# Finer modulation units in the opening, and two modulation sums moved from ahead of the attention to behind it

## The reference, cut to what matters

```python
ml = (silu(c) @ mod_w[i] + mod_b[i])            # 6 * 1024 columns a layer
sh1, sc1, g1, sh2, sc2, g2 = split(ml, 6)
hl = xl * (1 + sc1) + sh1                       # latent tokens; hc likewise with c_ctx
q, k, v = split(h @ wqkv, 3)                    # rotary turn of q and k (latent)
y = diff_attention(q, k, v) @ wo                # 8 heads, two softmaxes a head
x = layer_norm(ALPHA * x + (1 + g1) * y)
x = layer_norm(ALPHA * x + (1 + g2) * moe(x * (1 + sc2) + sh2))
```

## Time and profile before

| | |
|---|---|
| median of 3 runs | 1204.79 us (1202.83 to 1206.70) |
| the profiled execution | 1203.59 us |
| its span | 1201.6 us, 12396 instructions, granted PE clock 0.985 |
| PE busy | 1134.2 us (94%) |
| DVE busy | 362.4 us (30%) |
| ACT busy | 166.6 us (14%) |
| read from memory | 476.18 MB, 397 GB/s over the span |

### The profile page before, as it was taken

How to read it: one execution, slowest core, us unless ns; L and a number is a source line. 1 busy time by engine, 2 the same in 40 slices (tenths; PEclk the granted TensorE clock), 3 DMA queues, 4 the chain that set the end, 5 groups by cost and what they waited for, 6 DMA issues and landing times.

```text
span 1201.6 us, 12396 instructions
## 1 busy us (share of the span) xinstructions
PE 1134.2 (94%) x5288; PEld 494.0 (41%) x5288; DVE 362.4 (30%) x732; ACT 166.6 (14%) x397; POOL 8.0 (1%) x10
## 2 busy tenths in 40 slices
PE   8997998898999999999999889999999999988986
PEld 3553554545444333343333227543333433333322
DVE  1559999673111121111111115212111111111113
ACT  1101233614100000001000005200000100000000
POOL 0000000000000000000000010000000000000000
PEclk9998999899999999999999999999999999999998
DMA  9999896983999999999999999999999999999994
GB/s 397 403 361 368 301 361 261 402 323 155 431 430 430 431 429 429 432 430 431 431 430 430 430 427 427 424 431 430 431 430 430 431 430 431 431 428 432 430 429 181
DMA packets 40441, 480.17 MB, mean 400 GB/s; under 512 B 5056, under 2 KB 6336, under 8 KB 8384
## 3 DMA queue, kind: packets, MB, share of 16 engines
q1 hardware_dynamic: 39328, 476.91, 94.6%
q10 hardware_dynamic: 1056, 2.43, 0.7%
HBM read 476.18 MB, written 1.05 MB: 397 GB/s over the span
## 4 chain that ended last, share of the span: by engine, by line
PE 69%; DMA 23%; DVE 6%; ACT 1%; issue 1%; another core or an unknown queue 0%; DVEq 0%; SPq 0%; ACTq 0%
PE ps L913 41%; DMA ring<-in_moe_wu 12%; DMA ring<-in_moe_wg 8%; PE ps L905 4%; PE ps L921 4%; DMA ring<-in_mod_w 3%; PE ps L662 3%; PE ps L762 2%; PE ps L665 2%; DVE ring L1350 1%; PE ps L725 1%; PE ps L668 1%; PE ps L743 1%; DVE modp L1350 1%; PE ps L578 1%; PE ps L931 1%
## 5 line engine op out<-in xcount | busy, mean ns | idle before, releaser
L913 PE MATMUL ps<-ring,tra 128*64 128x512 f32 x2048 | 454.1, 597 | 24.2 <-DMA ring<-in_moe_wu 19.2
L913 PEld LDWEIGHTS ps<-ring,tra 128*64 128x64 f32 x2048 | 147.5, 138 | 322.6 <-issue 280.8
L913 PE MATMUL ps<-ring,work 128*64 128x512 f32 x1024 | 226.8, 595 | 1.9 <-DVE work L1701 1.9
L913 PEld LDWEIGHTS ps<-ring,work 128*64 128x64 f32 x1024 | 71.6, 137 | 135.6 <-issue 133.3
L1240 ACT ACTIVATE work<-ps 128x512 f32<-128x512 f32 x32 | 19.1, 598 | 506.7 <-PE ps L913 506.7
L1699 DVE TENSOR_TENSOR work<-work,ps 128x512 f32<-128x512 f32 x32 | 22.0, 688 | 206.0 <-PE ps L913 206.0
L1233 ACT ACTIVATE tra<-ps,cols 128x128 f32<-128x128 f32 x128 | 48.2, 457 | 255.1 <-PE ps L905 255.1
L1696 DVE TENSOR_TENSOR work<-ps,work 128x512 f32<-128x512 f32 x32 | 22.1, 692 | 202.3 <-ACT work L1240 202.3
L905 PEld LDWEIGHTS ps<-extra,xn 128*128 128x128 f32 x512 | 61.0, 195 | 24.3 <-issue 22.7
L905 PE MATMUL ps<-extra,xn 128*128 128x128 f32 x512 | 66.9, 285 | 1.4 <-DVE extra L1609 1.4
L921 PE MATMUL ps<-work,extra 64*128 64x512 f32 x256 | 63.6, 615 | 1.6 <-DVE work L1705 1.6
(11 more groups left out here) (191 smaller groups left out, 730.2 us busy)
## 6 DMA issues: line engine op xcount, KB each, us to landing
ring<-in_moe_wg SPq DMA_DIRECT2D x64, 2048.0 KB, 29.8
ring<-in_moe_wu SPq DMA_DIRECT2D x63, 2048.0 KB, 29.8
ring<-in_moe_wd SPq DMA_DIRECT2D x63, 2048.0 KB, 30.0
ring<-in_mod_w SPq DMA_DIRECT2D x40, 1024.0 KB, 9.6
ring<-in_mod_w SPq DMA_DIRECT2D x4, 2048.0 KB, 18.2
ring<-in_attn_wqkv SPq DMA_DIRECT2D x4, 2048.0 KB, 11.3
ring<-in_attn_wo SPq DMA_DIRECT2D x2, 2048.0 KB, 10.9
ring<-in_tokens SPq DMA_DIRECT2D x2, 1024.0 KB, 16.1
```

The source lines that it names most:

```text
L913: last = mm(ps[SLOTS * h:SLOTS * h + SLOTS, b, :], lhs(k0 + k), w[:, k, h * NB:(h + 1) * NB], start=(k0 + k == 0), stop=(k0 + k == KT - 1) ...
```

## The change

- The first four modulation units no longer hold shift or scale of half of the features but both of a quarter (`shift_and_scale`). Tokens and first key unit are loaded in quarters, each behind its modulation unit. PE runs `quarter_group(g, part)` for the key groups 0 to 3, with the next unit's `mod_parts` and `mod_columns` between them; the query groups 4 and 5 follow whole.
- `EARLY_SUMS` is 6 instead of 8, the ten step sums are now 6 to 15, and four (16 to 19) stand behind the attention: 16 ahead of `job_out(3)`, 17 and 18 ahead of `job_out(4)`, 19 in `attention_norm`, where `rows_sum(1)` was; that one moves into `route`. Both first rotations stand ahead of sum 5.
- `row_batch` 1, 2 and 3 go behind the groups 13 and 17 and into step 11, `row_batch(4)` behind `project(1, 1)`.
- `LOADS` is reordered from ("wo", 0) on; five units of the first expert and one of the second are issued from it, between the loads of the last sums. Slots 1 and 3 change places in `FREE`.

```diff
-FREE = (10, 4, 8, 5, 9, 6, 7, 2, 3, 1, 0)
+FREE = (10, 4, 8, 5, 9, 6, 7, 2, 1, 3, 0)
-BATCH_AT = {6: 0, 10: 1, 15: 2, 19: 3}
-EARLY_SUMS = 8
+BATCH_AT = {6: 0, 13: 1, 17: 2, 21: 3}
+EARLY_SUMS = 6
 STEP_SUMS = 10
+ROPES_AT = 5
 LOADS = [("q", 0), 0, 1, ("v", 0), 2, "rows", 3, 4, ("k", 1), 5, 6, 7, 8, ("q", 1), 9, "ahead", 10, 11, 12, ("v", 1), 13, 14,
-         ("wo", 0), 15, 16, 17, ("wo", 1), "x", 18, 19]
-AHEAD = 1
+         ("wo", 0), 15, ("wo", 1), "x", 16, 17, ("e", 1), ("e", 2), ("e", 3), ("e", 4), ("e", 5), 18, ("e", 6), 19]
+AHEAD, ISSUED = 1, 7
+def shift_and_scale(w):
+    import numpy as np
+    quarters = w[:, 0:2 * D].reshape(D, 2, 4, D // 4).transpose(0, 2, 1, 3).reshape(D, 2 * D)
+    return np.concatenate([quarters, w[:, 2 * D:]], 1)
...
-            for unit in (("mod", 0), ("mod", 2), ("k", 0), ("mod", 1), ("mod", 3)):
-                load_early(unit)
+            for i in range(4):
+                load_early(("mod", i))
+                c0, c1 = i * UNIT // 4, (i + 1) * UNIT // 4
+                load(slot(4)[:, c0:c1], tokens[:, c0:c1], sem(f"tokens_loaded_{i}"))
+                load(slot(0)[:, c0:c1], attn_wqkv[2][:, c0:c1], sem(f"first_loaded_{i}" if i < 3 else "early_loaded_0"))
...
-                elif v in (7, 8):
-                    sp.wait_ge(sem("half_summed"), 2 * (NSUM - 8 + v))
-                elif v < RING:
-                    sp.wait_ge(sem("unit_used"), NA - RING + v + 1)
+                elif v in (7, 9):
+                    sp.wait_ge(sem("half_summed"), 2 * (NSUM - 1 if v == 7 else NSUM))
+                elif v in (8, 10):
+                    early_used(sp, ("wo", (v - 8) // 2))
...
             mod_parts(0)
             keep_clock(7, 1)
             mod_columns(0)
-            keep_clock(7, 3)
-            mod_parts(1)
-            keep_clock(7, 1)
-            mod_columns(1)
-            keep_clock(4, 2)
+            keep_clock(5, 3)
...
+            for part in range(4):
+                quarter_group(0, part)
+                quarter_group(1, part)
+                if part < 3:
+                    mod_parts(part + 1)
+                quarter_group(2, part)
+                if part < 3:
+                    mod_columns(part + 1)
+                quarter_group(3, part)
+            for g in range(4, 10):
+                group(g)
...
-            row_batch(4)
-            NT_BANK = (4, 6, 5, 7)
+            NT_BANK = ((4, 6, 5, 0), (4, 6, 5, 7))
             project(1, 0)
             turn_normed(0, 0)
             project(1, 1)
-            pe.wait_ge(sem("rows_ready"), 2)
+            row_batch(4)
...
             for n in range(EARLY_SUMS):
-                if n == 6:
-                    rope_batch(0)
+                if n == ROPES_AT:
+                    for batch in range(2):
+                        rope_batch(batch)
                 unit_sum(n)
-            rope_batch(1)
...
+            unit_sum(NSUM - 4)
             job_out(3)
             heads_variance(1)
             norm_heads(1)
-            for n in range(EARLY_SUMS + STEP_SUMS, NSUM):
-                unit_sum(n)
+            unit_sum(NSUM - 3)
+            unit_sum(NSUM - 2)
             job_out(4)
...
                     if t == 0:
-                        rows_sum(1)
+                        unit_sum(NSUM - 1)
```

More of the change, by code:

```diff
@@ L52 @@
 BAND = P + 8
-PHASE_A = ([("mod", m) for m in (0, 2, 1, 3)]
+PHASE_A = ([("mod", i) for i in range(4)]
            + [(k, j) for j in range(2) for k in ("k", "q", "v")] + [("wo", 0), ("wo", 1)])
@@ L150, in laid_out @@
     given["router_w"] = router.reshape(P, KT * 32)
-    given["mod_w"] = np.stack([in_units(w) for w in given["mod_w"]])
+    given["mod_w"] = np.stack([in_units(shift_and_scale(given["mod_w"][0])), in_units(given["mod_w"][1])])
     w = given["attn_wqkv"][0]
@@ L437, in load_early @@
                 s, _ = EARLY[unit]
[L438 to L444, removed]
-            for unit in (("mod", 0), ("mod", 2), ("k", 0), ("mod", 1), ("mod", 3)):
-                load_early(unit)
+                load(slot(s), src, sem(f"early_loaded_{s}"))
+            for i in range(4):
[3 more added lines that the diff above has]
+                load(slot(0)[:, c0:c1], attn_wqkv[2][:, c0:c1], sem(f"first_loaded_{i}" if i < 3 else "early_loaded_0"))
             load(small9[:, 0:512], rope, sem("attn_small_loaded"))
@@ L505, in load_expert @@
             def load_expert(layer, e):
-                for n in range(AHEAD if layer == e == 0 else 0, EU):
-                    load_unit(layer, e, n)
+                for n in range(EU):
+                    if first_unit(layer, e) + n >= ISSUED:
+                        load_unit(layer, e, n)
             for what in LOADS:
@@ L516, in _ @@
                     load(xn[:, :].rearrange("p (t n) -> p t n", t=TT), x[0].rearrange("(t p) n -> p t n", p=P), sem("x_loaded"))
+                elif isinstance(what, tuple) and what[0] == "e":
+                    load_unit(0, what[1] // EU, what[1] % EU)
                 elif isinstance(what, tuple):
@@ L610, in mod_parts @@
                         k = 4 * r + g
-                        last = mm(bank((0, 1, 4, 5)[i], 32 * g, 32 * g + 32), cs[:, 32 * k:32 * k + 32], w[:, k, :],
+                        last = mm(bank(4 + i % 2, 32 * g, 32 * g + 32), cs[:, 32 * k:32 * k + 32], w[:, k, :],
                                   start=(r == 0), stop=(r == 1), skip_group_check=True)
@@ L615, in mod_columns @@
             def mod_columns(i):
-                bk = (2, 3, 6, 7)[i]
+                bk = 6 + i % 2
                 pe.wait_ge(sem("modp_copied"), i + 1)
+                if i >= 2:
+                    pe.wait_ge(sem("hcol_ready"), i - 1)
                 for q in range(4):
@@ L670, in multiply, with quarter_group @@
                 return last
[L672 to L676, removed]
-                else:
[L678 to L682, removed]
+            def quarter_group(g, part):
+                if part < 3:
+                    pe.wait_ge(sem(f"first_loaded_{part}"), 16)
+                else:
+                    early(("k", 0))
+                pe.wait_ge(sem("lat_ready"), 2 * part + 2)
+                pe.wait_ge(sem("ctx_ready"), 2 * part + 2)
+                for k in range(2 * part, 2 * part + 2):
                     last = multiply(g, k)
-                if part == 1:
+                if part == 3:
                     finish(g, last)
@@ L1089, in _ @@
                 turn_weights().then_inc(sem("sw_turned"), 1)
+                if layer == 0:
+                    pe.wait_ge(sem("rows_ready"), 2)
                 gather(7, 1).then_inc(sem("gather_done"), 1)
@@ L1312, in _ @@
             dve.wait_ge(sem("hbias_loaded"), 16)
[L1314 to L1319, removed]
+            v_.tensor_scalar(hb[:, 1], hb[:, 1], 1.0, None, ALU.add).then_inc(sem("hbias_ready"), 1)
+            dve.wait_ge(sem("hbias_ready"), 1)
             for i in range(4):
-                m = PHASE_A[i][1]
+                h, q = i // 2, 2 * (i % 2)
                 early_used(dve, PHASE_A[i])
@@ L1325, in _ @@
                     dve.wait_ge(sem("hcols_done"), i - 1)
-                v_.tensor_copy(sums[i % 2], bank((0, 1, 4, 5)[i])).then_inc(sem("modp_copied"), 1)
+                v_.tensor_copy(sums[i % 2], bank(4 + i % 2)).then_inc(sem("modp_copied"), 1)
                 dve.wait_ge(sem("hcols_done"), i + 1)
[L1328 to L1335, removed]
+                v_.tensor_tensor(hcol[:, :, h, q:q + 2, :], bank(6 + i % 2, 0, 8).rearrange("p (w q c) -> p w q c", w=2, q=2),
+                                 hb[:, :, h, q:q + 2].unsqueeze(3).to_broadcast([P, 2, 2, 2]), ALU.add).then_inc(sem("hcol_ready"), 1)
+                dve.wait_ge(sem("hcol_ready"), i + 1)
+                dve.wait_ge(sem(f"tokens_loaded_{i}"), 16)
+                for k in range(2 * i, 2 * i + 2):
+                    h_ = hT[:, k, 0:TOK]
+                    v_.tensor_scalar(h_, h_, hcol[:, 1, h, k % 4, 0:1], hcol[:, 0, h, k % 4, 0:1], ALU.mult, ALU.add)\
+                        .then_inc(sem("lat_ready"), 1)
             def half_sum(i):
@@ L1623, in route @@
                     normed_out(layer, t)
+                if layer == 0:
+                    rows_sum(1)
                 dve.wait_ge(sem("logits_done"), layer + 1)
```

23 lines of the change are left out of this document (12 added, 11 removed).

## The result

The changed kernel takes 1210.84 us in the median of 5 runs (1206.45 to 1212.06), against 1204.79 before: ratio 1.0051, 95% interval [1.0039, 1.0064]. It is slower by 0.5%. Its profiled execution has a span of 1209.7 us, 8.1 longer than before. Taken once more beside other kernels it gave 1210.26 us, ratio 1.0053 [1.0036, 1.0070].

What follows compares the result with a forecast made beforehand. The prediction took the end to hang on when the first expert starts, with transfers saturated from 300 us on. Terms of 0.7 and 1.4 us made 2.1 us later, 1206.9 us in the median; range 1200 to 1212.

Steps and rivals of the forecast that it cites:

- The likeliest case: Whole kernel: 2.1 us later than before, 1206.9 us in the median, given 44%.
- The wait named as the one that decides: PE waits 11.3 us ahead of group 16 for the load of ("v", 1).
- signs of being right: First scores near 102.6 us, ("v", 1) issued near 147.5, maximum of step 9 near 200, DVE waiting for mod_w near 246.
- Opening: From the kernel's start to the value groups: they start at 65.6 us, 3.4 earlier.
- Ahead of the attention: From value groups to first scores: scores at 102.6 instead of 113.04 us, 12 us won with the slow clock gone.
- The unit ("v", 1): Attention up to step 9: load issued at 147.5, landed at 160.7 us; all that was won is gone, and 0.7 us more.
- no wait at all: Rival ahead of group 16: the unit's issue is not bound by sum 10; 1194.2 us, chance 13%.
- The disputed landing: Load of ("v", 1) ahead of group 16: taken to land 13.2 us after issue, against 9.2 by the Trainium skill's rule.
- Steps 9 to 15: Late attention, with row_batch(3) waiting for sum 15 in step 11: taken as 0, bounds -1.5 and +1.9 us.
- Behind the attention: Last sums and projection: sum 18's load stands behind ("e", 5), so project(1, 0) starts 1.4 us later, bounds 0 and 3.5.
- Slower: the clock falls in the new gaps: Rival: PE's clock drops in both new gaps, up to 1.9 us each; 5.9 us later, 1210.7 us, chance 25%.
- the two gaps named: PE's new waits at row_batch(3) and at project(1, 0), about 2 us each.

Runs made afterwards that it cites:

- e9_copies_later: The changed kernel with the four ACT copies for the first keys held back until those for the first queries: 1203.32 us, ratio 0.9992 to the kernel before.
- e2_batch_later: The changed kernel with row_batch(0) behind group 7 instead of group 6: 1203.73 us, ratio 0.9997 to the kernel before.
- e1_v1_early: The changed kernel with the load of ("v", 1) moved in LOADS from behind sum 12 to behind sum 10: 1197.38 us, ratio 0.9955 to the kernel before.
- e11_copies_behind: The changed kernel with the four ACT copies of the second queries issued behind group 16 instead of group 15: 1207.01 us, ratio 1.0017 to the kernel before.
- the moved sums alone: The kernel before with the change's sums, rotations, collecting and load order, but its old opening by halves: 1207.45 us, ratio 1.0032 to the kernel before.
- e10_four: The changed kernel with ("v", 1) loaded earlier, row_batch(0) a group later, sums 18 and 19 loaded ahead of ("e", 5) and ("e", 6), row_batch(3) a step later: 1191.27 us.
- the study's fastest kernel: The changed kernel with ("v", 1) loaded earlier, row_batch(0) a group later, sums 18 and 19 loaded ahead of ("e", 5) and ("e", 6): 1189.21 us, ratio 0.988.

## Why the prediction was right and wrong

The likeliest case said 2.1 us later, less than the 0.3% that could be told from no change; it is 6 us later, inside the range of 1200 to 1212 and clearly slower. The wait named as the one that decides is there and is the largest; the step that failed is the one ahead of it, and that the range held is in part luck. By the prediction's own sign of being wrong, a first expert that starts more than 4 us from its old place, it was wrong: the expert starts 8.2 us later in the first profile and 5.7 in the second. Of the signs of being right the wait of some 11 us and DVE's wait for mod_w came as told, the latter 10 us later; the first scores, the issue of the unit and the maximum of step 9 are 4 to 7 us late. Up to that maximum, in the first profile, 5.8 us of the 7.4 above the forecast come from the first scores and 1.5 from the landing.

*Opening.* Forecast 65.6 us for the value groups, measured 65.66 (65.5 to 66.6 in the other traces with this opening). Right, including that the small pieces cost nothing on PE.

*Ahead of the attention: the step that failed.* "`row_batch(0)` needs sum 3, done at 70.68 + 3.11 = 73.8 us: 1.2 us of new wait", and from it first scores at 102.6 us. I had carried sum 3's end over from the kernel before as if its transfers could not be later. But the new opening finishes the key groups before it begins the query groups, where before the change the first halves of all six ran ahead of the second halves. So it moves ACT's four copies of the first keys forward by 10 us, in front of the transfers of sum 2. ACT's queue before and after the change:

```profile
62.95 2.54 ACTq L1104 DMA_DIRECT2D ring<-ring  x4
```
```profile
52.73 2.58 ACTq L1106 DMA_DIRECT2D ring<-ring  x4
```

`e9_copies_later` shows that they are the cause. Sum 3 ended at 76.6, the wait was 4.0 us (3.1 in the second profile), and PE's clock fell behind it in both: eight matmul instructions took 5.90 and 5.29 us instead of 3.60. Of the clock I had counted nothing. First scores at 108.4 and 106.3 us; without that wait 101.2 to 102.2, which is near the place forecast. In time it is worth 6.5 to 7 us (`e2_batch_later`, `e9_copies_later`): without this wait the kernel is level with the one before, at ratios 0.9997 and 0.9992.

*The unit ("v", 1).* Right in mechanism: the load goes out behind sum 10, and PE waits ahead of group 16. From the first scores to this issue I had 147.5 - 102.6 = 44.9 us; measured 45.2. The landing, taken as 13.2, was 14.7 and 13.7. The wait, forecast as 11.3, was 12.75 and 11.74. The slow clock cost 1.7 and 1.9 (forecast 1.9). `e1_v1_early` shows that this wait alone costs 12 to 13 us of time; the case "no wait at all" was false of the change, but is what the edit of one entry makes of it.

*The disputed landing.* With copies beside it 12.4 to 14.7 us in all ten traces in which the unit is issued behind sum 12, without 9.5 (`e11_copies_behind`), as the rows 12.5, 14.0 and 9.4 of the earlier trace rows had it. The rule of the Trainium skill ("DMA: Bandwidth & Descriptors", "Anatomy of one DMA"), an estimate of 9.2 us for the two transfers, agrees with the 9.5 and not with the others. The page gives it for transfers that GpSimd issues; these loads are issued by SP. The same page of the Trainium skill, under "Issuing engines are not separate DMA queues", says that transfers issued by different engines interleave on the same DMA engines, and these traces agree: with ACT's copies beside it SP's load took at least 12.4 us, without them 9.5.

*Steps 9 to 15.* Taken as 0. `row_batch(3)` waited 2.1 us; behind the wait its eight instructions took 1.89 us in the first profile (granted clock 0.53), and the full-speed 1.07 in two others, the moved sums alone and `e11_copies_behind`. The projection starts 8.7 us late where the maximum of step 9 was 8.2 late, so these steps cost 0.6 us; in the second profile they gave back 1.0. `e10_four` shows that the wait only changes its name when the collecting goes.

*Behind the attention.* Sum 18's late load: forecast 1.4 us at `project(1, 0)`, measured 0.7 (17.26 against 16.55 us from the first block's start) and 1.1 in the second profile. Too large by 0.3 to 0.7 us, and right in place. Sum 19, `row_batch(4)` and `rows_sum(1)` are hidden: `project(1, 0)` was 9.4 us late, the first expert 8.2. In the second profile these are 5.4 and 5.7. The difference is the slow stretch at L905 in the route, of which the forecast has nothing; it is in eight of the twelve traces of kernels with the moved sums and in neither of the other two. What brings it about was not tried.

*The rivals.* "Slower: the clock falls in the new gaps" came half true in the changed kernel, in one of the two gaps named, and at places that it did not name (behind the wait ahead of `row_batch(0)`, and in the route of the second profile). With the moved sums alone it fell in the other gap named too: `project(1, 0)` took 8.80 us behind a wait of 2.04. It was the right side of the range for a partly wrong reason. The prediction says that no row shows a gap of 2 us with a slow stretch behind it; the trace of the kernel before has one near the end of the attention, where the granted clock is 1.00 from 227 to 229 us and 0.50 from 230 to 232, and eight instructions that elsewhere take 1.06 us take 2.05. First that row, then `project(1, 0)` with the moved sums alone:

```profile
230.08 2.05 PE L743 MATMUL ps<-ring,tra 128*128 128x128 f32 x8 [1.76 <-ACT ring L1179]
```
```profile
257.25 8.80 PE L766 MATMUL ps<-ring,tra 128*128 128x512 f32 x16 [2.04 <-issue]
```

## What to carry to other kernels

When work is moved to a later place, look for what is queued behind its loads: here a unit of attention weights stood in one hand-written queue behind a load that waits for a moved sum, and moving that one entry is worth 12 to 13 us. When an earlier part becomes faster or its order changes, what it issues comes at other times too, small copies among them; do not keep the landing times of the kernel before for transfers that they will now meet. And a collecting step put exactly where its input used to be ready has no slack left: here, one group later, it ran without a wait.

## What the runs showed that I had not expected

The four copies of 128 KB are 0.5 MB, which at 430 GB/s is 1.2 us. They lengthened the landing of one 2 MB load by 2.9 to 5.2 us (12.4 to 14.7 against 9.5) and made sum 2 begin 0.6 to 3.9 us later (59.09 to 62.43 against 58.50). Why copies inside the chip lengthen a load by two to four times what their bytes would take was not tried and stays open.

The clock after short waits of PE is the other. From the start of `row_batch(0)` to the first scores, PE's work takes 28.7 us where there was no wait (72.79 to 101.45). Behind waits of 2.44, 3.13 and 3.99 us it took 30.2, 30.3 and 31.7. And the wait of 2.10 us ahead of `row_batch(3)`, alike in every kernel with the moved sums but `e10_four`, was followed by 1.07 us for its eight instructions in two traces and by 1.17 to 1.94 in the nine others. In the study's fastest kernel, where the waits ahead of `row_batch(0)` and of group 16 are gone, the four executions lie within 1.2 us, against 5.6 for the first five of the changed kernel. With `row_batch(3)` a step later they lie 3.7 apart without those waits, so it is not shown that the spread comes from them.
